# Two products of 64 keys on column halves for one of 128 keys, in the recurrence of the second block's mixers

## The chip, the core and the metric

The kernel is one program on one core of a Trainium2 chip. The metric is the device time of one execution in microseconds; lower is better. Engines: PE is TensorE, DVE is VectorE, ACT is ScalarE, POOL is GpSimd, SP issues the DMAs. One execution was taken by the hardware profiler.

## What is computed

Two transformer blocks on 512 tokens of 1024 features. The first mixes tokens in four ways and has a mixture of experts; the second has two hybrid layers. Each hybrid layer projects its input once and feeds three mixers, differential attention, a gated linear recurrence (HGRN2) in both directions, and attention on a memory, then an output projection and a convolved feed-forward. The change touches the recurrence:

```python
def step(state, inp):
    qt, kt, vt, bt = inp
    o_inter = jnp.einsum('bhtk,bhkv->bhtv', qt * jnp.exp(bt), state)
    diff = bt[:, :, :, None, :] - bt[:, :, None, :, :]
    dec = jnp.where(mask, jnp.exp(jnp.where(mask, diff, 0.0)), 0.0)
    attn = jnp.einsum('bhtk,bhtsk->bhts', qt, dec * kt[:, :, None, :, :])
    o_intra = jnp.einsum('bhts,bhsv->bhtv', attn, vt)
    b_last = bt[:, :, -1:, :]
    state = jnp.exp(b_last[:, :, 0, :])[..., None] * state + jnp.einsum(
        'bhsk,bhsv->bhkv', kt * jnp.exp(b_last - bt), vt)
    return state, o_inter + o_intra
```

There are 4 heads of 128 features each. The second direction runs the same on the flipped sequence.

## The kernel before, in words

`mixers` (L2947) runs once for each of the two layers. The sequence is cut into 4 chunks of 128 tokens. Within a chunk the 128x128 matrix `attn` of each head is built in rounds, since the decay depends on both tokens and on the feature. Round 0 (`round0`, L3178) makes scores for tokens that lie in the same block of 4. Level i (`level`, L3189; i = 1 to 5) makes them for pairs of tokens in the two halves of a block of 2, 4, ... times 4 tokens, so of 8, 16, 32, 64 and 128 tokens, with the decay taken against the block's middle: half_of(i) is 4, 8, 16, 32, 64. In the forward direction (d = 0) the queries are the upper half of a block and the keys the lower one; backward (d = 1) it is the other way round.

For each chunk and head, a round is one product in float32: stationary are the weighed keys of the whole chunk (128 features x 128 keys), moving are the weighed queries (128 in round 0, the 64 of the query side in a level). The result goes to `lev`, called `L` in the code, four PSUM banks of 128x512. A float32 product is two passes, so 16 products are 32 pairs of LDWEIGHTS and MATMUL. A level uses two of the four banks, alternately. DVE then copies with a mask what belongs to the level into `att` (`keep0` L3859, L3865; `keep`, L3878); what lies outside the mask in the banks is computed and not used.

The order of the work is written out by hand for every engine. On PE, between rounds, stands one tile of the input projection, w_in (`tile(n)`, L3138, L3139 and L3144: 24 passes of 128x512 in fp32r), because the recurrence leaves PE waiting otherwise:

```python
round0(0); turn_values(0); tile(10)
for i in range(1, 6):
    level(0, i)
    if i < 4: turn_values(i)
    tile(10 + i)
for h in range(H): turn_keys(0, h)
```

Backward the same stands with `rot(i)` (L3247, one product of the rotary position code) in place of `turn_values`, tiles 21 to 25. `turn_keys` (L3214) and `turn_values` (L3175) are transposes against the identity. DVE's order per level is: `far(d, i+1)` (L3842, L3843: differences of the cumulated decay; they wait for the level that last read that buffer), `weigh(d, i)` (L3857, L3858: keys and queries times the decay; `weigh0` is L3849, L3850), `keep(d, i-1)`, `low_part(n)` (L3779: the low part of a weight tile, which `tile(n)` needs for its last third and which waits for `tile(n-2)`); backward `rope` is added (L3918, L3919, L3921), which waits for the product of `rot` and lets the next `rot` go on. ACT takes each tile's result (L3513), makes the high part of a later one (L3503), and makes the exponentials (L3530 to L3546). After level 5 come `to_end` on DVE (L3884, L3885), an exponential on ACT (L3545, L3546) and `weigh_ends` on DVE (L3889, L3890), on which `turn_keys` waits. `clamp(0)` (L3813, L3814) stands early in the mixers, some 30 us ahead of round 0. SP loads w_in in blocks of 512 KB into a ring of three.

The prediction also reads two places outside the change: `new_state` of the first block's recurrence (L1574, L1575), whose products have 64 stationary and 64 moving columns and whose heads write PSUM partitions 0 to 63 and 64 to 127 in turn, and `token_means` (L3263), whose products have 32 stationary columns and write the four strips of 32 partitions in turn.

Of the kernel before, what the change touches and what calls it, by code (L numbers as in the profile page):

```python
# [14 lines left out]
P = 128  # L15
# [151 lines left out]
@contextmanager  # L167
def stage(nc, *names):

    with ExitStack() as ctx:  # L170
        sems = [ctx.enter_context(nc.semaphore(n)) for n in names]
        with nc.Block() as block:
            yield (block, *sems)
        nc.clear_and_free_semaphores(sems)
        nc.all_engine_barrier()
# [180 lines left out]
def parts_of(K, x, n=S):  # L356

    with ExitStack() as ctx:
# [6 lines left out]
NORM_SEMS = ["x_mean", "x_centred", "x_squared", "x_var", "x_root", "x_inverse", "x_spread", "x_scaled", "x_biased",  # L365
             "x_high", "x_low"]


EARLY_SEMS = ["e_summed", "e_shift", "e_prepared", "e_centred", "e_squared"]
# [2577 lines left out]
def mixers(K, a, layer, x, cs, sn, gain, bias):  # L2947
# [5 lines left out]
    nc = K.nc  # L2953
    lam_init = 0.8 - 0.6 * float(np.exp(-0.3 * layer))
    share = 1.0 - lam_init
    with ExitStack() as ctx:
# [6 lines left out]
        with ExitStack() as c1:  # L2963
# [28 lines left out]
            L = K.ps(c1, "lev", [P, 4, 512])  # L2992
# [5 lines left out]
            z = [quad["z0"], quad["z1"], quad["z2"]]  # L2998
# [50 lines left out]
            def half_of(i):  # L3049
                return 4 << (i - 1)  # L3050

            def query_side(ap, i, d):

                return ap.rearrange("p g (n two m) -> p g n two m", two=2, m=half_of(i))[:, :, :, 0 if d else 1, :]
# [6 lines left out]
            def blocks(t, m):  # L3061
# [7 lines left out]
                     "a_gathered", "a_summed", "a_stored", "m_scored", "m_max", "m_exps", "m_mixed", "m_turned", "m_gathered",  # L3069
                     "m_summed", "m_stored", "d_squared", "d_mean", "d_root", "d_normed",  # L3070
                     "mv_turned", "mv_taken", "yh_ready", "yl_ready", "eps_ready", "w_taken", "positions_in",
                     "turned", "rope_ready"] + EARLY_SEMS + NORM_SEMS
            with stage(nc, *names) as (block, *sems):
                (loaded0, loaded1, loaded2, mem_in, high_ready, low_ready, product, taken, lam_prod, lam_sum,
                 lam_exp, own, lb_diff, lb_ready, gate_in, clamped, logs, k_ready, q_ready, offset, decay,
# [3 lines left out]
                 a_gathered, a_summed, a_stored, m_scored, m_max, m_exps, m_mixed, m_turned, m_gathered,  # L3079
                 m_summed, m_stored, d_squared, d_mean, d_root, d_normed,  # L3080
                 mv_turned, mv_taken, yh_ready, yl_ready, eps_ready, w_taken, positions_in,
                 turned, rope_ready), norm_sems = sems[:-len(NORM_SEMS) - len(EARLY_SEMS)], sems[-len(NORM_SEMS):]
                early = Early(K, x, 6, K.mu[:, :], K.spare[:, :], lambda j: kk[j // 4][:, j % 4, :], sems[-len(NORM_SEMS) - len(EARLY_SEMS):-len(NORM_SEMS)])
                norm = Norm(K, x, gain, bias, X0[:, :], X1[:, :], lambda j: xsq[j // 4][:, j % 4, :], turned_t[:, 0:P],
                            norm_sems, high, low)
# [38 lines left out]
                def _(pe):  # L3124
# [52 lines left out]

                    def round0(d):  # L3178
                        pe.wait_ge(decayed, 14 * d + 2)
                        if d:  # L3180
                            pe.wait_ge(state_ready, 3)
                            pe.wait_ge(put_f, 4)
                        for c in range(NT):
                            s = slice(c * P, (c + 1) * P)
                            for h in range(H):
                                mm = nc.tensor.matmul(L[:, c, h * P:(h + 1) * P], z[1][:, h, s], z[0][:, h, s], start=True, stop=True)
                            mm.then_inc(matched, 1)

                    def level(d, i):  # L3189
                        zz = z[(i + 1) % 3]  # L3190
                        zq = query_side(zz[:, :, :], i, d)
                        n64 = 64 // half_of(i)
                        pe.wait_ge(decayed, 14 * d + 2 + 2 * i)
                        pe.wait_ge(kept, 14 * d + (4 if i < 3 else 2 * i))
                        for j in (0, 1):
                            for cc in (0, 1):
                                c = 2 * j + cc
                                for h in range(H):
                                    g = (cc * H + h) * 64
                                    mm = nc.tensor.matmul(L[:, 2 * (i % 2) + j, g:g + 64], zz[:, h, c * P:(c + 1) * P],  # L3200
                                                          zq[:, h, c * n64:(c + 1) * n64, :], start=True, stop=True)
                            mm.then_inc(matched, 1)

                    def turn_keys(d, h):
# [210 lines left out]
                    for n in range(FIRST_TILES, 10):  # L3415
                        tile(n)
                    round0(0)
                    turn_values(0)
                    tile(10)
                    for i in range(1, 6):  # L3420
                        level(0, i)
                        if i < 4:
                            turn_values(i)
                        tile(10 + i)
# [9 lines left out]
                    rot(0)  # L3434
                    tile(20)
                    round0(1)
                    for i in range(1, 6):
                        level(1, i)
                        rot(i)
                        tile(20 + i)  # L3440
# [330 lines left out]
                def _(dve):  # L3771
                    step = Own(dve, own)

                    def low_part(n):
                        if n >= given:
                            dve.wait_ge(high_ready, n + 1 - given)
                        if n >= 2:
                            dve.wait_ge(product, n - 1)
                        nc.vector.tensor_tensor(wl[:, n % 2, 0:unit_width(n)], raw_of(n), high_of(n), ALU.subtract).then_inc(low_ready, 1)  # L3779
# [20 lines left out]
                    def clamp(d):  # L3800
                        if d:
                            dve.wait_ge(gate_in, 1)
                            dve.wait_ge(k_turned, 4)
                            dve.wait_ge(decay, 10)
                        else:
                            dve.wait_ge(taken, 4)
                        if layer:
                            dve.wait_ge(lb_ready, 1)
                            for h in range(H):
                                step.go(nc.vector.tensor_scalar(kk[d][:, h, :], kk[d][:, h, :], lb[:, 1, d, h:h + 1], lb[:, 0, d, h:h + 1],  # L3810
                                                                ALU.mult, ALU.add))
                            step.all()
                        nc.vector.tensor_scalar(b[:, :, :], kk[d][:, :, :], 2.0 ** -60, None, ALU.max).then_inc(clamped, 1)  # L3813
                        nc.vector.tensor_scalar(z[2][:, :, :], kk[d][:, :, :], 1e-20, 2.0 ** -60, ALU.max, ALU.min).then_inc(clamped, 1)  # L3814
# [188 lines left out]
                        rope_quarter()  # L4003
                    low_part(5)
                    clamp(0)
                    dve.wait_ge(lam_exp, 1)
                    step(nc.vector.tensor_tensor(neglam[:, 0:1], neglam[:, 1:2], neglam[:, 0:1], ALU.subtract))
                    step(nc.vector.tensor_scalar(neglam[:, 0:1], neglam[:, 0:1], lam_init, None, ALU.subtract))
# [389 lines left out]
def second_block(K, a, x, out):  # L4398
    with ExitStack() as ctx:
        cs = K.sb(ctx, "cs", [P, S])  # L4400
        sn = K.sb(ctx, "sn", [P, S])
        K.spare = K.ps(ctx, "x_var", [P, S])
        for layer in range(2):
            first = (lambda t: K.col("ln_in_g_2", t), lambda t: K.col("ln_in_b_2", t))
            later = (lambda t: K.col("ln2_g_2", t), lambda t: K.col("ln2_b_2", t))
            mixers(K, a, layer, x, cs, sn, *(later if layer else first))
            feed_forward(K, a, layer, x, lambda t: K.col("ln1_g_2", 8 * layer + t), lambda t: K.col("ln1_b_2", 8 * layer + t))
        last_norm(K, x, lambda t: K.col("ln2_g_2", 8 + t), lambda t: K.col("ln2_b_2", 8 + t), out)
# [73 lines left out]
```

## Time and profile before

| | us |
|---|---|
| median of 3 runs | 3530.47 (3528.61 to 3533.96) |
| profiled execution, its span | 3526.3 |
| median less that span | 4.2 |
| PE busy | 3363.8 (95%) |
| DVE busy | 2510.4 (71%) |
| ACT busy | 1906.0 (54%) |

The span reaches from the first to the last instruction of the one execution that was profiled; what lies around it in a measured run is not in the profile, so that execution's own time is known only as its span. The mean granted TensorE clock was 0.969 of full speed over the span. A busy PE means that matmuls are in flight; they are pipelined, so the spacing of their starts says more than their durations.

### The profile page before, as it was taken

How to read it: one execution, taken by the hardware profiler on the slowest of the kernel's cores; microseconds unless marked ns; L12 is line 12 of the kernel's file. 1: busy time of each engine (PE TensorE's matmuls, PEld its weight loads, DVE VectorE, ACT ScalarE, POOL GpSimd, SP SyncE). 2: the span in 40 equal slices, each digit the busy share in tenths (PEclk: the TensorE clock that was granted, in tenths of full speed). 3: DMA queues.
4: the chain of work that ended last, by engine and by line, in shares of the span. 5: the costliest groups of instructions: out<-in, count | busy, mean ns of one | idle time of the engine just before them, and what ended most of it. 6: DMA issues, size and time to landing. Idle time of an engine off the chain costs nothing. (4 is left out here: it accounts for less than half of the span.)

```text
span 3526.3 us, 45471 instructions
## 1 busy us (share of the span) xinstructions
PE 3363.8 (95%) x16942; PEld 2708.0 (77%) x16942; DVE 2510.4 (71%) x2900; ACT 1906.0 (54%) x2152; POOL 241.4 (7%) x202
## 2 busy tenths in 40 slices
PE   8998987999999999999989998999999999899998
PEld 6886665888888888888758886778887887678886
DVE  6654566999999999999757766566536775656543
ACT  4223334778777877778646536344415534534422
POOL 0000000122121212121100000000000000000000
PEclk9998997999999999999979999999999999999999
DMA  4110236999999999999812110223331111023331
GB/s 151 49 31 27 64 117 238 363 367 368 365 370 363 369 364 369 369 368 367 291 39 84 60 61 29 68 84 96 107 97 65 62 55 59 24 86 96 97 108 65
DMA packets 118802, 600.28 MB, mean 170 GB/s; under 512 B 20722, under 2 KB 24194, under 8 KB 68130
## 3 DMA queue, kind: packets, MB, share of 16 engines
q1 hardware_dynamic: 105346, 580.93, 45.4%
q0 software_dynamic: 13312, 17.35, 2.0%
q8 instruction: 100, 1.64, 0.2%
q14 instruction: 44, 0.36, 0.0%
HBM read 586.06 MB, written 28.90 MB: 174 GB/s over the span
## 5 line engine op out<-in xcount | busy, mean ns | idle before, releaser
L2486 DVE TENSOR_TENSOR wl<-raw,wh 128x2048 fp32r<-128x2048 f32 x384 | 872.7, 2286 | 52.0 <-ACT wh L2415 52.0
L2415 ACT ACTIVATE wh<-raw 128x2048 fp32r<-128x2048 f32 x384 | 735.6, 1916 | 189.0 <-PE pu L2360 144.4
L2358 PE MATMUL pu<-wh,Xh 128*128 128x512 f32 x1024 | 409.7, 400 | 0.0
L2360 PE MATMUL pu<-wh,Xl 128*128 128x512 f32 x1024 | 399.9, 391 | 0.0
L2359 PE MATMUL pu<-wl,Xh 128*128 128x512 f32 x1024 | 399.8, 390 | 0.0
L4300 ACT ACTIVATE w_high<-w_raw 128x1024 fp32r<-128x1024 f32 (+1 forms) x114 | 131.3, 1151 | 320.4 <-PE acc L4272 161.1
L4347 DVE TENSOR_TENSOR w_low<-w_raw,w_high 128x1024 fp32r<-128x1024 f32 (+1 forms) x114 | 152.4, 1337 | 185.3 <-PE ps L4230 100.0
L4252 PE MATMUL ps<-x_high,w_high 128*128 128x512 f32 x656 | 255.2, 389 | 0.0
L4253 PE MATMUL ps<-x_low,w_high 128*128 128x512 f32 x656 | 255.2, 389 | 0.0
L2358 PEld LDWEIGHTS pu<-wh,Xh 128*128 128x128 f32 x1024 | 192.7, 188 | 45.4 <-issue 8.1
L2360 PEld LDWEIGHTS pu<-wh,Xl 128*128 128x128 f32 x1024 | 192.6, 188 | 42.0
L2359 PEld LDWEIGHTS pu<-wl,Xh 128*128 128x128 f32 x1024 | 193.0, 188 | 37.2
L3138 PE MATMUL acc<-x_high,w_high 128*128 128x512 f32 x528 | 218.5, 414 | 1.5 <-ACT hq L3513 1.5
L2358 PE MATMUL pd<-wh,hh 128*128 128x512 f32 x512 | 208.8, 408 | 0.2 <-DVE hl L2500 0.2
L3139 PE MATMUL acc<-x_low,w_high 128*128 128x512 f32 x528 | 207.6, 393 | 0.0
L2360 PE MATMUL pd<-wh,hl 128*128 128x512 f32 x512 | 200.3, 391 | 0.0
L2359 PE MATMUL pd<-wl,hh 128*128 128x512 f32 x512 | 199.6, 390 | 0.0
L4230 PE MATMUL ps<-x_high,w_low 128*128 128x512 f32 x704 | 173.2, 389 | 0.0
L3779 DVE TENSOR_TENSOR w_low<-w_raw,w_high 128x1024 fp32r<-128x1024 f32 (+1 forms) x102 | 115.6, 1135 | 57.9 <-PE acc L3144 28.3
L4230 PEld LDWEIGHTS ps<-x_high,w_low 128*128 128x128 f32 x704 | 132.1, 188 | 27.4
L4252 PEld LDWEIGHTS ps<-x_high,w_high 128*128 128x128 f32 x656 | 123.1, 188 | 25.6
L4253 PEld LDWEIGHTS ps<-x_low,w_high 128*128 128x128 f32 x656 | 123.1, 188 | 25.5
(784 smaller groups left out, 6837.8 us busy)
## 6 DMA issues: line engine op xcount, KB each, us to landing
raw<-in_exp_w SPq DMA_DIRECT2D x384, 1024.0 KB, 7.6
w_raw<-in_w_in SPq DMA_DIRECT2D x100, 512.0 KB, 3.4
w_raw<-in_w_up SPq DMA_DIRECT2D x82, 512.0 KB, 3.8
w_raw<-in_w_down SPq DMA_DIRECT2D x32, 704.0 KB, 4.0
w_raw<-in_w_out SPq DMA_DIRECT2D x32, 384.0 KB, 3.1
kv_raw<-in_w_mem_kv SPq DMA_DIRECT2D x16, 512.0 KB, 3.7
x<-in_x SPq DMA_DIRECT2D x4, 1024.0 KB, 8.2
w_raw<-in_w_out SPq DMA_DIRECT2D x8, 512.0 KB, 4.9
```

The lines of the kernel that those rows point to most:

```text
L2358: nc.tensor.matmul(o, lh[:, k, :], wh[:, m % PARTS, c], start=(m >= 8 and kh == 0 and kk == 0), stop=False)
L2359: nc.tensor.matmul(o, lh[:, k, :], wl[:, m % PARTS, c], start=False, stop=False)
L2360: mm = nc.tensor.matmul(o, ll[:, k, :], wh[:, m % PARTS, c], start=False, stop=end)
L2415: nc.scalar.activation(wh[:, m % PARTS, :], raw[:, m % RAW, :], ACT.Copy).then_inc(w_high, 1)
L2486: nc.vector.tensor_tensor(wl[:, m % PARTS, :], raw[:, m % RAW, :], wh[:, m % PARTS, :], ALU.subtract).then_inc(w_low, 1)
L3138: nc.tensor.matmul(o, wh[:, n % 3, c], high[:, k, :], start=(k == 0), stop=False)
L3139: nc.tensor.matmul(o, wh[:, n % 3, c], low[:, k, :], start=False, stop=False)
L4230: mm = nc.tensor.matmul(o, wl[:, u % 2, c], high[:, k, :], start=False, stop=(k == DT - 1))
L4252: nc.tensor.matmul(o, wh(u)[:, c], high[:, k, :], start=(k == 0), stop=False)
L4253: nc.tensor.matmul(o, wh(u)[:, c], low[:, k, :], start=False, stop=False)
L4300: nc.scalar.activation(wh(u), raw_of(u), ACT.Copy).then_inc(high_ready, 1)
L4347: nc.vector.tensor_tensor(wl[:, u % 2, 0:width(u)], raw_of(u), wh(u), ALU.subtract).then_inc(low_ready, 1)
```

## The change

Round 0 and levels 1 to 4 make, for each chunk and head, two products of 64 keys in place of one of 128: one with the keys 0 to 63 of the chunk, written to PSUM partitions 0 to 63, and one with the keys 64 to 127, written to partitions 64 to 127, each against only those queries that lie in the same half of the chunk (64 of 128 in round 0, 32 of 64 in a level). Level 5 makes one product of 64 keys: forward the lower half, backward the upper half, against the 64 queries of the other half. What a level wrote outside of that before is no longer written, and so DVE clears the first three banks of `lev` once in each layer, after `clamp(0)`; round 0 waits for it.

```diff
 def round0(d):
     pe.wait_ge(decayed, 14 * d + 2)
+    pe.wait_ge(lev_cleared, 1)
     if d:
         pe.wait_ge(state_ready, 3)
         pe.wait_ge(put_f, 4)
     for c in range(NT):
-        s = slice(c * P, (c + 1) * P)
         for h in range(H):
-            mm = nc.tensor.matmul(L[:, c, h * P:(h + 1) * P], z[1][:, h, s], z[0][:, h, s], start=True, stop=True)
+            for r in (0, 64):
+                s, g = slice(c * P + r, c * P + r + 64), h * P + r
+                mm = nc.tensor.matmul(L[r:r + 64, c, g:g + 64], z[1][:, h, s], z[0][:, h, s], start=True, stop=True)
         mm.then_inc(matched, 1)
...
                 for h in range(H):
                     g = (cc * H + h) * 64
-                    mm = nc.tensor.matmul(L[:, 2 * (i % 2) + j, g:g + 64], zz[:, h, c * P:(c + 1) * P],
-                                          zq[:, h, c * n64:(c + 1) * n64, :], start=True, stop=True)
+                    if i == 5:
+                        r = 64 * d
+                        mm = nc.tensor.matmul(L[r:r + 64, 2 * (i % 2) + j, g:g + 64], zz[:, h, c * P + r:c * P + r + 64],
+                                              zq[:, h, c:c + 1, :], start=True, stop=True)
+                        continue
+                    for side in (0, 1):
+                        r, b0 = 64 * side, c * n64 + side * n64 // 2
+                        mm = nc.tensor.matmul(L[r:r + 64, 2 * (i % 2) + j, g + 32 * side:g + 32 * side + 32],
+                                              zz[:, h, c * P + r:c * P + r + 64], zq[:, h, b0:b0 + n64 // 2, :],
+                                              start=True, stop=True)
             mm.then_inc(matched, 1)
...
     clamp(0)
+    nc.vector.memset(L[:, 0:3, :], 0.0).then_inc(lev_cleared, 1)
     dve.wait_ge(lam_exp, 1)
```

## Rows read from the trace of the kernel before

**Rows 1.** The page, its first part: busy time and share of the span.

```profile
PE 3363.8 (95%) x16942; PEld 2708.0 (77%) x16942; DVE 2510.4 (71%) x2900; ACT 1906.0 (54%) x2152; POOL 241.4 (7%) x202
```

**Rows 2.** Windows, forward then backward: PE, PEld, DVE, ACT, POOL, clock, DMA, GB/s.

```profile
1937.00:1947.00 10.00, 10.00 (x64) 8.95 (x63) 6.23 (x7) 3.95 (x4) 0.00 (x0) 1.00 0.18 52
...
2020.00:2030.00 10.00, 10.00 (x60) 8.48 (x59) 9.93 (x12) 3.85 (x4) 0.00 (x0) 1.00 0.15 54
```

**Rows 3.** Timeline, forward, layer 0: start, length, engine, line; round 0, level 1.

```profile
1909.28 3.73 PE L3186 MATMUL lev<-z,z 128*128 128x128 f32 x32
...
1912.85 0.60 PE L3175 MATMUL x_mu<-const,hout 128*128 128x128 f32 x4
...
1918.78 3.68 PE L3200 MATMUL lev<-z 128*128 128x64 f32 x32
```

**Rows 4.** Timeline of the first block's recurrence: products of 64 columns.

```profile
279.29 0.29 PE L1575 MATMUL G<-vt,ktt 128*64 128x64 f32 x4
...
279.41 0.33 PE L1574 MATMUL G<-x,btt 128*64 128x64 f32 x4
...
279.53 0.33 PE L1575 MATMUL G<-vt,ktt 128*64 128x64 f32 x4
```

**Rows 5.** Timeline, layer 1: from transposes to narrow products and back.

```profile
2927.70 0.60 PE L3258 MATMUL x_mu<-const,dv 128*128 128x128 f32 x4
...
2928.23 0.81 PEld L3263 LDWEIGHTS lev<-z,const 128*32 128x32 f32 x32 [0.17 <-issue]
...
2929.24 0.50 PE L3138 MATMUL acc<-x_high,w_high 128*128 128x512 f32 x1
...
2929.58 0.39 PE L3139 MATMUL acc<-x_low,w_high 128*128 128x512 f32 x1
```

**Rows 6.** Timeline, backward direction, layer 0: levels 1 to 5, DVE's weighing.

```profile
2010.88 3.76 PE L3200 MATMUL lev<-z 128*128 128x64 f32 x32 [2.02 <-DVE att L3865]
...
2020.76 3.65 PEld L3200 LDWEIGHTS lev<-z 128*128 128x128 f32 x32 [0.16 <-DVE z L3858]
...
2028.41 1.22 DVE L3858 TENSOR_TENSOR z<-hfb,z 128x1024 f32<-128x1024 f32 x1
...
2030.54 3.77 PEld L3200 LDWEIGHTS lev<-z 128*128 128x128 f32 x32
...
2037.34 1.22 DVE L3858 TENSOR_TENSOR z<-hfb,z 128x1024 f32<-128x1024 f32 x1
...
2040.46 3.77 PEld L3200 LDWEIGHTS lev<-z 128*128 128x128 f32 x32
...
2050.38 3.77 PEld L3200 LDWEIGHTS lev<-z 128*128 128x128 f32 x32
...
2050.88 1.23 DVE L3779 TENSOR_TENSOR w_low<-w_raw,w_high 128x1024 fp32r<-128x1024 f32 x1 [5.64 <-PE acc L3144]
...
2056.35 1.10 PE L3247 MATMUL x_var<-dk,const 128*128 128x512 f32 x2 [2.06 <-DVE rope_t L3918]
```

**Rows 7.** Layer 1, backward: a window with its granted clock; levels 1, 2 (timeline).

```profile
2843.30:2850.20 6.90, 6.90 (x24) 5.51 (x24) 6.83 (x9) 4.45 (x4) 0.00 (x0) 0.51 0.23 76
...
2841.51 5.40 PE L3200 MATMUL lev<-z 128*128 128x64 f32 x32 [2.04 <-DVE att L3865]
...
2854.54 3.77 PEld L3200 LDWEIGHTS lev<-z 128*128 128x128 f32 x32
```

**Rows 8.** Timeline, forward, layer 0: weigh_ends and the first turn_keys.

```profile
1959.86 2.29 DVE L3889 TENSOR_TENSOR z<-hff,z 128x2048 f32<-128x2048 f32 x1 [4.89 <-ACT ends L3546]
...
1965.24 1.03 PE L3214 MATMUL lev<-const,z 128*128 128x128 f32 x8
```

**Rows 9.** Timeline, DVE around clamp(0) in both layers, and a PSUM copy.

```profile
1879.71 0.16 DVE L4007 TENSOR_TENSOR neglam<-neglam 128x1 f32<-128x1 f32 x1 [3.18 <-ACT neglam L3642]
...
1911.90 2.59 DVE L3865 COPY_PREDICATED att<-const,lev 128x512 f32<-128x512 int32 x4
...
2715.40 2.29 DVE L3818 TENSOR_TENSOR sums<-sums,z 128x2048 f32<-128x2048 f32 x1 [2.28 <-ACT z L3522]
```

More of the change, by code:

```diff
@@ L3071, in mixers @@
                      "mv_turned", "mv_taken", "yh_ready", "yl_ready", "eps_ready", "w_taken", "positions_in",
-                     "turned", "rope_ready"] + EARLY_SEMS + NORM_SEMS
+                     "turned", "rope_ready", "lev_cleared"] + EARLY_SEMS + NORM_SEMS
             with stage(nc, *names) as (block, *sems):
@@ L3081, in mixers @@
                  mv_turned, mv_taken, yh_ready, yl_ready, eps_ready, w_taken, positions_in,
-                 turned, rope_ready), norm_sems = sems[:-len(NORM_SEMS) - len(EARLY_SEMS)], sems[-len(NORM_SEMS):]
+                 turned, rope_ready, lev_cleared), norm_sems = sems[:-len(NORM_SEMS) - len(EARLY_SEMS)], sems[-len(NORM_SEMS):]
                 early = Early(K, x, 6, K.mu[:, :], K.spare[:, :], lambda j: kk[j // 4][:, j % 4, :], sems[-len(NORM_SEMS) - len(EARLY_SEMS):-len(NORM_SEMS)])
```

## The prediction, made before the changed kernel was run

> **What bounds the kernel now.** The page gives PE (TensorE) as busy 95% of the span of 3526.3 us [rows 1]. That share is an average over many stages, so I read the stage that the change touches, the mixers' recurrence, once in each of the two layers. The stage by stage windows tell two different stories [rows 2]: in the forward direction PE is busy all of the 10 us and DVE 6.23 us of them; in the backward one, where DVE also does the rotary work, DVE is busy 9.93 of 10 us. So the forward stages should pay in full, the backward ones only until DVE holds PE back.
>
> **What a stage costs now.** A round or level is 32 pairs of weight load and matmul (16 products in float32, two passes each). Round 0 has its first matmul at 1909.28 and the first matmul of the next stage is at 1912.85: 3.57 us for 32 pairs, 112 ns a pair. The levels stream half as many columns per matmul and take as long: 3.68 us from the first matmul's start to the last one's end, against 3.73 in round 0 [rows 3]. The streamed columns therefore don't set the pace, the 128-column weight load does.
>
> **What a stage will cost.** Round 0 and levels 1 to 4 get 64 pairs of 64 columns, alternately on the lower and upper column half; level 5 gets 32 pairs, all on one half. The nearest rows are a product of the first block, with 64 stationary and 64 moving columns, whose heads go to column halves in turn [rows 4]. There groups of four matmuls start at 279.29, 279.41 and 279.53: 0.12 us for four pairs, 30 ns each. One half alone would then pace at about 60 ns, the other filling in between. I take 30 ns: 64 pairs are 1.9 us; level 5's 32 pairs on one half at 60 ns are 1.9 us as well. Levels stream 32 columns instead of 64, for which no row exists; since the load sets the pace I give that nothing. The bounds per stage are 1.6 us (32 narrow pairs over four strips have their loads done in 0.81 us [rows 5], 25 ns each) and 3.8 us (64 pairs at 60 ns, no overlap between halves).
>
> **What the switch costs.** Before, the first load of a level hid behind the tile's last matmul. Narrow column tiles break the stream. Where transposes over the full array give way to 32-column products, the last wide matmul starts at 2927.70+3x0.11 = 2928.03 and the first narrow one at 2928.23; the spacing before was 0.11, so 0.09 us is lost [rows 5]. On the way back the wide matmul starts at 2929.24 with its load (0.50 us long instead of 0.39) and its successor comes 0.34 us later instead of 0.23: a second 0.09 and an unhidden load of 0.11. With the 64-column load, half of that, unhidden on entry: 0.09+0.06+0.09+0.11 = 0.35 us per stage. Zero and 0.6 us bound it, since the semaphore wait in the same place may be part of the 0.20. A stage falls from 3.57 to 1.92+0.35 = 2.27 us, a gain of 1.3 us. The Trainium skill speaks against the change just here: by "TensorEngine Tiling (Array Packing)", Key Properties, changing the tiling mode drains TensorE. The trace agrees, with the 0.09 us above on either side; were there no drain, the sum would be some 3 us better.
>
> **Forward, both layers.** Six stages (round 0, five levels) of 1.3 us are 7.9 us a layer. What must keep ahead: DVE's 6.23 us of work in 10 leave more room than the 1.3 us by which a stage shrinks, and in DVE's order each weighing stands about a stage ahead of the level that reads it (in the first two stages DVE is full, and lives on that lead). The tightest is the chain at the end: tile(14)'s result on ACT, then the exponential, then weigh_ends, which waits 4.89 us for ACT today; its first half is done at 1959.86+2.29 = 1962.15, and turn_keys, which needs it, starts its matmuls at 1965.24 [rows 8]. That chain moves with tile(14) and turn_keys by one stage more, so of the 3.1 us some 1.8 are left. The DMA queues bring one block of 512 KB per stage and are idle most of the time. Two layers: 15.8 us.
>
> **Backward, layer 0.** Levels 1 to 3 hang on DVE. Level 1 waits 2.02 us for keep0 today and still starts at 2010.88 (all times here less the forward gain); level 2, whose loads start at 2020.76, still waits for the weighing, 0.16 us today [rows 6]. From then on a PE period is (2040.46-2030.54)-1.3 = 8.6 us, and DVE's is 2037.34-2028.41 = 8.93 us. Level 3 starts when DVE's weighing ends, 2028.41+1.22 = 2029.63, not at 2030.54: 0.9 gained; level 4 at 2038.6 instead of 2040.46: 1.9; level 5, which has no far step before it on DVE, at 2047.2 instead of 2050.38: 3.2 us. What follows is clocked by tile(24)'s end: DVE waits 5.64 us for it, then keep(1,4), to_end and rope(4), for which PE's rot(5) waits 2.06 us [rows 6]. Level 5's own gain only lengthens that wait. So 3.2 us.
>
> **Backward, layer 1.** Here the granted clock fell to 0.51 from 2843.3 to 2850.2 (1.2 GHz; PE had just stood waiting for keep0) and level 2 starts at 2854.54 [rows 7]: 833.8 us after layer 0's 2020.76, where level 1, at 2841.51 and 2010.88, is 830.6 us apart; so the fall cost 3.2 us [rows 6, 7]. DVE then has slack, PE is the bound, and levels 1 to 4 give 1.3 us each: 5.3 us.
>
> **The clearing and the waits.** The new memset writes 1536 columns of PSUM from DVE. No row has it; four PSUM copies of 512 columns took 2.59 us [rows 9], so 1.9 us by that, 0.5 us at the least. In layer 0 it lands in a 3.18 us idle of DVE; in layer 1 DVE has 2.28 us of idle a little later and only one weight split between [rows 9], which tile(6) needs at about the time when it will be ready. I take nothing; 0 to 1 us. PE's new wait in front of round 0 is met some 30 us before (the memset follows clamp(0), at the 3.18 us idle at 1879.71), so what queues behind it on PE loses nothing. The 640 more instructions per layer are given nothing.
>
> **Sum.** 15.8+3.2+5.3 = 24.3 us. Against that, PE's idle before level 1 and before rot(5) grows from 2.1 to about 3.5 us, and in layer 1 either idle of today was followed by the low clock; in layer 0 neither was. I deduct 1.5 us for one such fall more. Net 23 us. The profiled execution's span is 3526.3 us and the runs' median 3530.5, 4.2 us of it outside the span, which stays: 3530.5-23 = 3507.5 us.
>
> **Rivals.**
> (B) The halves don't overlap in this order (two passes low, two high, and so on; in the block of [rows 4] four and four). Then a stage of 64 costs 3.8+0.35 us, 0.6 more than today, and level 5 saves 1.3. A layer loses 2x(5x0.6-1.3) = 3.4 us at most, part of it in PE's idle: 3533 us, within the noise. Against it stand the 30 ns of [rows 4] and the 32 pairs in 0.81 us of [rows 5]. 7%. By the Trainium skill, "TensorE: Matmul & The Clock Gate", Wait — 56ns, not 53.3ns?, a sequencer in its ucode mode spends about 62 ns on every MATMUL, whatever its size; by that this would be 3540 us, an estimate. The 30 ns of [rows 4] contradict it.
> (C) Slower: every change of half drains as a change of mode does. Place: 31 changes in each of ten stages a layer. At 0.09 us each a stage costs 2.27+2.8 = 5.1 us, 1.5 more than today; forward 5x1.5-1.3 = 6.2 us, backward some 5 us after PE's idle is used up, both layers about 22 us: 3553 us. It decides from 1.3/31 = 0.042 us per change. For it: a switch that costs 0.09 exists. Against it: the products of [rows 5] change strips at every product, at 25 ns a pair. 4%.
> (D) The backward stages give nothing, by falls of the clock in the longer idles of both layers or by DVE: forward alone, 3514.7 us. For it: the full DVE of [rows 2] and the fall of [rows 7]. 12%.
> (E) Cheaper switches and pairs (no switch cost, 1.7 us a stage): 1.9 us a stage, 22.8 forward and some 11 backward: 3497 us. 10%.
> My forecast has the remaining 67%.
>
> **How the numbers follow.** The likeliest case gives 3507.5. The range 3497 to 3522 takes in D and E, a switch of 0.6 us a stage (0.25 us more in some 20 stages that bind, 5 us), the memset's 1 us and two falls of the clock; B and C lie outside. A measurement can tell about 0.2%, 7 us, from no change. Faster by more than that: A, D, E, 89% less what a sum of small misses takes, 0.88. Within: B, 0.08. Slower: C and B's worse half, 0.04.
>
> **What would show it.** In the new profile the 64-column loads of round 0 and levels should show about 0.14 us, a stage of 64 pairs about 2 us, level 5 the same with half the pairs; a gap of 0.2 us on either side of each; level to level 8.1 us forward where it was 9.4, and about 8.9 backward in layer 0 with new short waits for DVE; weigh_ends still ahead of turn_keys; the memset under 2 us within DVE's idle. A stage of 4 us would be B, of 5 us C. A forward gain per layer under 6 us would make the switch cost wrong; more low clock around the idle before level 1 and rot(5) would be D.

## The result, and the profile after

| | before | changed |
|---|---|---|
| median | 3529.54 us (4 runs) | 3503.28 us (4 runs, 3501.45 to 3505.52) |
| span of the profiled execution | 3526.3 us | 3500.6 us |
| ratio of the runs | | 0.9922 (95% interval 0.9908 to 0.9936) |

The kernel became 26.3 us faster by the medians and 25.7 us by the profiled spans; 3507.5 us was forecast, in a range of 3497 to 3522. In the page, the head answers to [rows 1]. What stands behind the levels in the code has line numbers 10 higher than before (11 behind the clearing); a level is now L3209 (levels 1 to 4) and L3204 (level 5), round 0 is L3188, turn_keys L3224.

```profile
span 3500.6 us, 46757 instructions
PE 3331.6 (95%) x17582; PEld 2668.4 (76%) x17582; DVE 2512.5 (72%) x2902; ACT 1905.5 (54%) x2152; POOL 240.7 (7%) x202
```

PE carries 640 more pairs of weight load and matmul and is busy 32 us less, while its share of 95% hasn't moved: that number says nothing of a stage.

The timeline of the changed kernel, forward, layer 0, answers to [rows 3]; before a name stand start, length, engine and line:

```profile
1905.31 1.97 PE L3144 MATMUL acc<-x_high,w_low 128*128 128x512 f32 x8
...
1907.21 2.08 PE L3188 MATMUL lev<-z,z 128*64 128x64 f32 x64
...
1909.22 0.66 PE L3175 MATMUL x_mu<-const,hout 128*128 128x128 f32 x4
...
1915.30 2.06 PE L3209 MATMUL lev<-z 128*64 128x32 f32 x64
...
1954.72 1.03 PE L3224 MATMUL lev<-const,z 128*128 128x128 f32 x8
```

Round 0 has twice the pairs. From its first matmul's start to its last one's it takes 1.86 us (the 2.08 us less the last matmul's own 0.22), where it took 3.46; that is 29.5 ns a pair. From its first matmul to the next stage's is 2.01 us, against 3.57. The eight wide matmuls ahead of it start 0.227 us apart, the last at 1905.31+7x0.227 = 1906.90, so the entry takes 0.31 us where the stream has 0.23. Levels stream half as many columns and take 2.06 us against 2.08: here too the load sets the pace, not the streamed columns. The last line is the first turn_keys, 47.51 us after round 0, where it was 55.96 us.

The windows answer to [rows 2]:

```profile
1937.00:1947.00 10.00, 10.00 (x100) 8.15 (x98) 6.79 (x7) 3.35 (x3) 0.00 (x0) 1.00 0.21 60
...
2010.00:2020.00 10.00, 9.87 (x123) 7.67 (x121) 9.93 (x13) 4.41 (x5) 0.00 (x0) 1.00 0.15 54
```

In the forward window PE is still never idle and DVE has room. The backward timeline, layer 0, answers to [rows 6]:

```profile
2000.35 2.95 PE L3209 MATMUL lev<-z 128*64 128x32 f32 x64 [3.58 <-DVE att L3875]
...
2017.88 1.22 DVE L3868 TENSOR_TENSOR z<-hfb,z 128x1024 f32<-128x1024 f32 x1
...
2019.15 2.06 PE L3209 MATMUL lev<-z 128*64 128x32 f32 x64
...
2028.10 2.06 PE L3209 MATMUL lev<-z 128*64 128x32 f32 x64 [0.36 <-DVE z L3868]
...
2036.64 2.08 PE L3204 MATMUL lev<-z 128*64 128x64 f32 x32
...
2036.81 1.23 DVE L3789 TENSOR_TENSOR w_low<-w_raw,w_high 128x1024 fp32r<-128x1024 f32 x1 [2.05 <-PE acc L3144]
...
2042.28 2.05 PE L3257 MATMUL x_var<-dk,const 128*128 128x512 f32 x2 [3.57 <-DVE rope_t L3928]
...
2051.16 1.04 PE L3224 MATMUL lev<-const,z 128*128 128x128 f32 x8
```

Levels 3 and 4 start as DVE's weighing ends (2017.88+1.22 = 2019.10), 8.95 us apart, DVE's period. DVE's wait for tile(24) fell from 5.64 to 2.05 us, and PE's wait for rope(4) grew from 2.06 to 3.57 us, just as level 5 shrank.

Where the time went, from the starts of the first matmuls in both traces, in us after the start of round 0 of the same direction and layer:

| | before | changed | gain |
|---|---|---|---|
| forward, to turn_keys, layer 0 | 55.96 | 47.51 | 8.45 |
| backward, to level 5, layer 0 | 45.48 | 41.95 | 3.53 |
| backward, to turn_keys, layer 0 | 58.92 | 56.47 | 2.45 |
| forward, to turn_keys, layer 1 | 55.96 | 47.51 | 8.45 |
| backward, to level 5, layer 1 | 48.79 | 41.95 | 6.84 |
| backward, to turn_keys, layer 1 | 63.40 | 57.67 | 5.73 |

The four stretches to turn_keys give 25.1 us. The remaining 0.6 us lies outside: round 0 of layer 0 already starts 2.1 us earlier than before, and the stretches behind turn_keys give 1.4 us of that back. The early start is no work of the change: in the eleven traces of this case the first round 0 starts anywhere from 1904.1 to 1913.0 us.

The clearing is one memset, in the timeline of DVE in layer 0, and DVE's wait for ACT after it in layer 1 (both answer to [rows 9]):

```profile
1874.68 1.34 DVE L4016 MEMSET lev<- 128x1536 f32 x1 [0.32 <-issue]
...
1877.55 0.16 DVE L4018 TENSOR_TENSOR neglam<-neglam 128x1 f32<-128x1 f32 x1 [1.52 <-ACT neglam L3652]
...
2702.71 2.29 DVE L3828 TENSOR_TENSOR sums<-sums,z 128x2048 f32<-128x2048 f32 x1 [0.64 <-ACT z L3532]
```

It took 1.34 us, with 0.32 us ahead of it. DVE's idle shrank by both together, from 3.18 to 1.52 us in layer 0 and from 2.28 to 0.64 us in layer 1: hidden in both.

### The profile page after: what moved, and what is told of

It is laid out like the page before. It is cut to its first block and busy times, and to the rows that moved or that the text cites. A ratio compares the mean times of both kernels' runs of the same rounds, so it can differ in the third digit from the quotient of the medians.

```text
span 3500.6 us, 46757 instructions
## 1 busy us (share of the span) xinstructions
PE 3331.6 (95%) x17582; PEld 2668.4 (76%) x17582; DVE 2512.5 (72%) x2902; ACT 1905.5 (54%) x2152; POOL 240.7 (7%) x202
```

## The experiments

The code of each is the changed kernel with the edit shown, unless it says otherwise. The medians of the kernel before in the three sets of runs were 3530.06, 3533.39 and 3532.55 us, so across sets the ratios, each to the kernel before, compare better than the times. Times after round 0 are read from one trace of each kernel.

**All of one half, then all of the other.** The same products in another order, in the levels 1 to 4 too. DVE is told of a bank only when its upper half is done.

```diff
-for c in range(NT):
-    for h in range(H):
-        for r in (0, 64):
+for r in (0, 64):
+    for c in range(NT):
+        for h in range(H):
             s, g = slice(c * P + r, c * P + r + 64), h * P + r
             mm = nc.tensor.matmul(L[r:r + 64, c, g:g + 64], ...)
...
```

> The changed kernel with the products of a round or level in another order: first all on the lower column half, then all on the upper one; the same products, the same loads. Theory (what pays is that the two halves run side by side): 32 pairs in a row on one half pace at about 58 ns, so a stage of 64 pairs takes 2 x 1.86 = 3.7 us in place of 1.9, a forward level-to-level period about 9.9 us in place of 8.06, and the whole about 3531 us. Rival (a 64-column product costs about 29 ns by itself, in any order): 1.9 us a stage and 3503 us, unchanged.

Measured: 3529.11 us, ratio 0.9996 (0.9984 to 1.0009); the whole gain is gone. The timeline, round 0 forward:

```profile
1904.09 3.77 PE L3188 MATMUL lev<-z,z 128*64 128x64 f32 x64
```

The same 64 pairs take 3.77-0.22 = 3.55 us in place of 1.86; forward turn_keys stands 55.80 us after round 0 in place of 47.51. Halving the load alone gives nothing, because there are twice as many loads. What pays is that the halves run side by side, and in this order they hardly do. Only at the seam do they overlap: in the single starts, where each half makes a series of its own some 58 ns apart, the first upper matmul is at 1905.777, ahead of the last three lower ones (1905.829, 1905.888 and 1905.946). That is also why the stage took 3.55 and not 3.7 us, and the forward period 9.72 rather than 9.9 us. Orders in between, with groups of 4 or 8 products to a half, were not run.

**Level 5 alone.** Round 0 and levels 1 to 4 with 128 keys.

```diff
+if i < 5:
+    mm = nc.tensor.matmul(L[:, 2 * (i % 2) + j, g:g + 64], zz[:, h, c * P:(c + 1) * P],
+                          zq[:, h, c * n64:(c + 1) * n64, :], start=True, stop=True)
+    continue
 if i == 5:
...
```

> Only level 5 is changed (one product of 64 keys on one half); round 0 and levels 1 to 4 as before the change. Theory (half the columns to load, half the time, and a switch of 0.35 us): level 5 takes 1.9+0.35 us, 1.4 us less than before in both forward directions; backward the level is followed by a wait for DVE and gives nothing. Together 2.8 us less than before: 3526.7 us. Rival (one half alone gains nothing, as the other stands idle): level 5 takes 3.6 us or more and the whole 3530 us.

Measured: 3528.7 us, ratio 0.9992 (0.9981 to 1.0004), which alone can't be told from nothing. The trace can: forward turn_keys stands 54.58 us after round 0 in both layers, 1.38 us less than before. The level in its timeline:

```profile
1959.05 2.08 PE L3207 MATMUL lev<-z 128*64 128x64 f32 x32
```

32 pairs in 1.86 us, 60 ns each: one half's own pace, as forecast. The rival, that one half alone gains nothing, is out.

**One wide product inside each narrow stage.** Round 0 and levels 1 to 4, chunk 1, head 3.

```diff
+if c == 1 and h == 3:
+    s = slice(c * P, (c + 1) * P)
+    mm = nc.tensor.matmul(L[:, c, h * P:(h + 1) * P], z[1][:, h, s], z[0][:, h, s], start=True, stop=True)
+    continue
 for r in (0, 64):
...
```

> The changed kernel, but one of the 16 products of round 0 and of levels 1 to 4 (chunk 1, head 3) is again one of 128 keys, so that each of these stages goes from the halves to the full array and back once more. Theory (a switch of the tiling drains and leaves one load unhidden, 0.35 us for in and out): 0.35+0.22-0.12 = 0.45 us more per stage, a forward period of 8.5 us in place of 8.06, 4 to 8 us more in all (3507 to 3511 us). Rival (the gaps beside the stages are semaphore waits, not drains): 0.1 us more per stage, 3504 us.

Measured: 3512.01 us, ratio 0.9940 (0.9921 to 0.9959). Round 0's timeline:

```profile
1906.10 1.04 PE L3192 MATMUL lev<-z,z 128*64 128x64 f32 x28
...
1907.07 0.30 PEld L3188 LDWEIGHTS lev<-z,z 128*128 128x128 f32 x2
1907.07 0.49 PE L3188 MATMUL lev<-z,z 128*128 128x128 f32 x2
1907.48 1.01 PEld L3192 LDWEIGHTS lev<-z,z 128*64 128x64 f32 x32
1907.48 1.15 PE L3192 MATMUL lev<-z,z 128*64 128x64 f32 x32
```

Then level 2:

```profile
1923.05 1.01 PE L3217 MATMUL lev<-z 128*64 128x32 f32 x28
1923.99 0.44 PE L3207 MATMUL lev<-z 128*128 128x64 f32 x2
1924.35 1.13 PE L3217 MATMUL lev<-z 128*64 128x32 f32 x32
```

In round 0 the last narrow matmul ahead of the island starts at 1906.10+1.04-0.22 = 1906.92, the island 0.15 us after it, and the next narrow one 0.41 us after the island begins, of which two wide pairs are 0.22. There is no semaphore wait in between, so the gaps belong to the switch, and the rival is out. The price depends on the stage. A level period is 8.42 us in place of 8.06: 0.36 us, less the 0.22 and plus the 0.12 of the four narrow pairs left out, 0.26 us for in and out. From round 0 to level 1 it is 8.53 us in place of 8.09: 0.44 us, and by the same sum 0.34 us, about the 0.35 assumed. The two differ in the streamed columns, 64 (128 in the wide product) against 32 (64): the pace of the pairs doesn't show them, the switch does. Forward turn_keys comes 1.9 us later in each layer. The interval of the ratio overlaps that of the changed kernel (0.9908 to 0.9936), so it is the trace that shows the price, not the time.

**Forward only.** The backward direction with 128 keys.

```diff
+if d == 1:
+    mm = nc.tensor.matmul(L[:, 2 * (i % 2) + j, g:g + 64], zz[:, h, c * P:(c + 1) * P],
+                          zq[:, h, c * n64:(c + 1) * n64, :], start=True, stop=True)
+    continue
...
```

> The forward direction as changed, the backward direction with products of 128 keys as before. Theory (forward PE is the bound and gains 1.4 us in each of six stages, backward DVE holds it back and gives some 2.5 us in layer 0 and 5.7 us in layer 1): 16.9 us less than before, 3512.6 us, 9 us more than the changed kernel. Rival (both directions give the same, 13 us each): 3516.5 us.

Measured: 3518.93 us, ratio 0.9967 (0.9954 to 0.9980), 6 us more than the theory gave, and 2 us more than the rival. Forward turn_keys stands at 47.51 us, exactly as in the changed kernel. It is the backward part, whose code is that of before, that came out slower than in the profile of before: 63.45 and 64.99 us to turn_keys where before had 58.92 and 63.40, 6.1 us in all. A window of it, layer 0, and level 1:

```profile
2000.00:2008.00 8.00, 8.00 (x35) 6.74 (x34) 7.93 (x10) 4.50 (x4) 0.00 (x0) 0.57 0.20 68
```

```profile
1999.26 5.84 PE L3207 MATMUL lev<-z 128*128 128x64 f32 x32 [2.03 <-DVE att L3883]
```

After the wait of 2.03 us the clock was at 1.2 GHz most of the window (0.57 granted) and level 1 took 5.84 us. Here the clock fell in both layers; in the trace of before it fell in one of two. So the backward direction with wide products varies by up to 4.5 us in a layer with the clock, and one profile of it isn't its price.

It isn't only the one trace: the median granted clock of the ten runs is 0.9665, against 0.969 in the 29 of the kernel before. By the medians the forward direction alone gives 11 us (7 to 16 by the interval), not the 16.9 us that its own stretches gained, and the backward direction on top of it gives some 16 us (0.9967-0.9922), not 8.2. Both splits add up to about the same whole. Whether a shorter forward direction makes the clock fall more often in a backward one with wide products, or whether it was chance, no run here tells.

**tile(25) before rot(5), backward.**

```diff
-for i in range(1, 6):
+for i in range(1, 5):
     level(1, i)
     rot(i)
     tile(20 + i)
+level(1, 5)
+tile(25)
+rot(5)
 rot(6)
```

> The changed kernel with one thing moved: backward, tile(25) runs before rot(5) in place of after it, so that PE has work while DVE makes to_end and rope(4). Theory (in the changed kernel the gain of backward level 5 is lost in PE's wait of 3.57 us before rot(5), which is also where the clock falls): the wait and the fall go, turn_keys comes some 2 to 4 us earlier after round 0 (56.5 and 57.7 us in the changed kernel) until it waits for weigh_ends and rot(6) for rope(5); 3 to 7 us less than the changed kernel, 3496 to 3500 us. Rival (DVE's chain from tile(24)'s end to weigh_ends sets turn_keys anyway): nothing, 3503 us.

Measured: 3508.43 us, ratio 0.9932 (0.9907 to 0.9958): no gain that can be told. turn_keys came at 56.08 and 56.23 us instead of 56.47 and 57.67. The wait only moved to rot(6), in the timeline of layer 0, and the low clock moved with it (0.72 granted from 2049 to 2055 us in layer 0, 0.50 from 2869 to 2875 in layer 1):

```profile
2049.30 1.94 PE L3257 MATMUL x_var<-dk,const 128*128 128x512 f32 x2 [3.84 <-DVE rope_t L3931]
```

rot(6) needs rope(5), which DVE makes behind weigh_ends. The theory's main part fell; the rival was nearly right.

**Strips of 32 keys.** Levels 1 to 3 are like round 0 below with 16 queries to a strip; level 4 makes two products, at `r = 64 * side + 32 * d`, of the 32 keys of each half that are used.

```diff
-for r in (0, 64):
-    s, g = slice(c * P + r, c * P + r + 64), h * P + r
-    mm = nc.tensor.matmul(L[r:r + 64, c, g:g + 64], z[1][:, h, s], z[0][:, h, s], start=True, stop=True)
+for r in (0, 32, 64, 96):
+    s, g = slice(c * P + r, c * P + r + 32), h * P + r
+    mm = nc.tensor.matmul(L[r:r + 32, c, g:g + 32], z[1][:, h, s], z[0][:, h, s], start=True, stop=True)
...
```

> The changed kernel, carried on: round 0 and levels 1 to 3 make four products of 32 keys on the four strips of 32 columns, level 4 two products of those 32 keys that are used in each half. Theory (four strips side by side, each paced by a 32-column load of 27 ns, so 7 ns a pair): 128 pairs in 0.9 us, a forward period of 7.1 us by PE, held at some 7.5 us by DVE's work in levels 1 to 3; 2.5 to 3.5 us less per layer forward, nothing backward; 3497 us. Rival (starting an instruction costs about 7 ns, two per pair): 14 ns a pair, 128 pairs in 1.8 us as now, 3503 us.

Measured: 3493.75 us, ratio 0.9892 (0.9864 to 0.9919). Timeline, round 0, then levels 1 and 4 forward:

```profile
1907.02 1.35 PE L3188 MATMUL lev<-z,z 128*32 128x32 f32 x128
...
1914.36 1.30 PE L3217 MATMUL lev<-z 128*32 128x16 f32 x128
...
1936.26 1.21 PE L3210 MATMUL lev<-z 128*32 128x32 f32 x64
```

128 pairs run in some 1.15 us, 9 ns each; 64 pairs on two strips in 1.01 us, 16 ns each. The 9 ns lie between the theory's 7 and the rival's 14, nearer to the theory. Forward turn_keys stands at 43.62 us, 3.9 us less than with halves, and the period is 7.30 us: DVE did not hold it back at 7.5, as it was expected to. Backward turn_keys came at 56.38 and 56.29 us in place of 56.47 and 57.67. The ratio's interval just overlaps that of the changed kernel.

**Tiles ahead of the levels, backward.**

```diff
 for i in range(1, 6):
+    tile(20 + i)
     level(1, i)
     rot(i)
-    tile(20 + i)
 rot(6)
```

> The changed kernel with the backward order turned round: each tile(20 + i) runs before level(1, i) and not after it. Theory (backward DVE is the bound once a level is short; PE then stands idle for DVE, and DVE in turn waits 2.05 us for tile(24)): PE's wait before level 1 is filled by tile(21), DVE's wait for tile(24) goes, turn_keys then waits for weigh_ends and for rot(6), some 4 us earlier in each layer; 3495 us. Rival (the backward direction is bound by PE as the forward one is): no change, 3503 us, or later, as the levels come later.

Measured: 3499.7 us, ratio 0.9914 (0.9884 to 0.9944). turn_keys stands at 54.11 us in both layers, 2.4 and 3.6 us less than in the changed kernel. The direction of the theory holds in the trace, where 4 us a layer were expected; the two ratios' intervals overlap, so the time alone doesn't show it.

**Both.**

> The two before together: strips of 32 keys, and tiles ahead of levels in the backward direction. If both theories hold their gains lie in different directions and add: 3489 us. If the backward one falls, 3497 us; if the strips give nothing, 3495 us.

Measured: 3490.82 us, where 3489 was expected if both hold, ratio 0.9876 (0.9854 to 0.9899), with turn_keys at 43.59 us forward and 54.17 backward. In the backward timeline PE now waits most for rope(5), before rot(6):

```profile
2042.21 2.05 PE L3271 MATMUL x_var<-dk,const 128*128 128x512 f32 x2 [5.67 <-DVE rope_t L3942]
```

**turn_keys before rot(6), added to the last one.**

```diff
-rot(6)
 for h in range(H):
     turn_keys(1, h)
+rot(6)
 tile(26)
```

> The kernel of the last run (strips of 32 keys, tiles ahead of levels backward) with rot(6) moved behind turn_keys. Theory (what PE waits for there, 5.67 us, is rope(5), which DVE makes only after weigh_ends, while turn_keys needs only the first half of weigh_ends): turn_keys starts some 49.5 us after round 0 in place of 54.2, 4 us less in each layer, 3482 us. Rival (what comes after is paced by DVE, which is as late as before): turn_keys earlier, the chunks not; 3490 us.

Measured: 3487.27 us, ratio 0.9875 (0.9858 to 0.9891). turn_keys comes at 49.3 us, as the theory says, and the first product of the chunks 68.3 and 68.7 us after round 0 in place of 70.9 and 71.9. The ratio is that of the run before it, so the time doesn't show whether the 2.6 and 3.2 us reach the end. The two traces say that they mostly do: from the first round 0 to the end is 1579.5 us there and 1574.5 us here, and what hides it in the spans is that round 0 started 6.7 us later, behind code that is the same in both. The forecast of 3482 us was 5 us too low. Either of the last two beats both kernels of this case by a margin clear of their intervals.

## Why the prediction was right, point by point

The likeliest case came about, in its mechanism forward and in layer 0 backward. In layer 1 the number was near partly by luck.

*What a stage costs.* The 30 ns a pair from [rows 4] were measured as 29.5, and level 5's 60 ns on one half as 60. Giving the 32 streamed columns nothing was right: levels and round 0 take the same. That the halves overlap, rival (B)'s question, is shown by the grouped order, which takes the whole gain away; what (B) feared came true in an order that the change doesn't have.

*The switch.* Mis-sized, the right way round: 0.35 us assumed. The island gives 0.26 us for in and out of a level and 0.34 us in round 0, and the forward period fell by 9.45-8.06 = 1.39 us, not 1.3. For a level the sum comes out as 3.52-1.87-0.26 = 1.39 us, where I had 3.57-1.92-0.35 = 1.3: 64 pairs take 1.87 us, and a wide level took 3.52 us to the next stage, not the 3.57 of round 0. Of what I put too high in the switch, 0.05 us is the return: I took the unhidden load of the 0.11 us that a wide fp32r tile shows in [rows 5], while behind a narrow stage forward come transposes, whose first matmul is only 0.33-0.27 = 0.06 us longer. "TensorEngine Tiling (Array Packing)" of the Trainium skill has it in Key Properties that changing the tiling mode drains TensorE. The 0.26 us agree in that the change has a price; whether it is a drain they don't tell. Rival (C), that each change of half drains, is out: 1.86 us with 31 changes.

*Forward.* 7.9 us a layer was forecast, 8.45 came; nothing on ACT or DVE got in the way, and even 7.30 us periods were kept.

*Backward, layer 0.* Levels 3 and 4 start when DVE's weighing ends and level 5 at 41.95 us, 3.5 us earlier (3.2 forecast). After PE's wait of 3.57 us the clock was then partly low (0.85 and 0.87 granted in the two windows of 6 us from 2038 on), rot(5) took 2.05 us where it took 1.10, and of the 3.5 us only 2.45 reached turn_keys. The sum had deducted 1.5 us for one such fall; this one cost 1.1.

*Backward, layer 1.* 5.3 us forecast, 5.7 measured to turn_keys, but not by the argued mechanism. I had let the loss of 3.2 us stand as an offset, taken DVE to have slack, and counted four stages of 1.3 us on PE. In fact level 5 gains 6.84 us: the clock fell here too (level 1 took 3.58 us), but a short level hides it, since DVE's weighing for level 2 ends only 15.49 us after round 0 in both layers. Level 2 starts 15.73 and 15.69 us after round 0, where before it was 15.74 and 19.03. From there on DVE holds levels 3 and 4 as in layer 0 (waits of 0.19 and 0.35 us). The timeline of levels 1 and 2 with the end of the weighing:

```profile
2820.44 3.58 PE L3209 MATMUL lev<-z 128*64 128x32 f32 x64 [3.59 <-DVE att L3875]
...
2829.04 1.22 DVE L3868 TENSOR_TENSOR z<-hfb,z 128x1024 f32<-128x1024 f32 x1
...
2830.45 0.72 PE L3209 MATMUL lev<-z 128*64 128x32 f32 x18
```

(The view ends within level 2.) Behind level 5 the clock was low again (0.50 granted from 2862 to 2868 us) and took 1.1 us back, a second fall that the sum didn't have. The two errors went opposite ways, so the near hit of this term is partly luck.

*The clearing.* Priced at 1.9 us by a PSUM copy, 1.34 measured (1.66 with what stands ahead of it), hidden as argued.

*The sum.* 24.3 less 1.5 was forecast, 25.1 measured over the four stretches, net of the clock. The differences: forward 1.1 us more, to level 5 backward 0.3 and 1.5 us more in layers 0 and 1, and 0.7 us more lost to the clock. This split goes by one trace of each kernel; by the medians of the forward-only kernel it is another, and that stays open.

## What to carry to other kernels

Where a product's stationary side is wide and its streamed side narrow, ask whether the load sets the pace: here 128 stationary columns took 110 to 112 ns a pair, with 64 as with 128 streamed columns. Splitting it into column parts paid when the parts alternated in the program, so that they ran side by side, and gave nothing when all of one part came first. Enter and leave such stages seldom: a visit cost 0.26 to 0.34 us. Before pricing a shorter stage, ask on the next engine whether it is already waited for: by the traces the forward direction gave the whole 8.45 us a layer, and the backward one 2.45 and 5.73 us. And where waits are followed by a low clock, don't take one trace for the price.

## What the runs showed of the hardware that was not expected

A half-width part paces at 58 to 60 ns a pair alone, two together at 29.5 ns; four strips of 32 columns at 9 ns a pair together, and two strips at 16 ns: the pace per strip rises only from 32 to 36 ns as four instead of two run.

Matmuls of different halves don't start in the order of the program: in the grouped kernel the first one of the upper half starts ahead of the last three of the lower half, which stand before it.

The low clock follows PE's waits in the backward direction, but not always. With the wait of some 2.0 us before level 1 it fell in five of eight passes (level 2 starting 19.0 us or more after round 0 in place of 15.7 or 15.8; the kernels before, grouped, level 5 only and forward only, two layers each). With the 3.6 us of the changed kernel it fell in both, and level 2 came at 15.7 all the same. That doesn't hold for every short level: with the wide island it came at 18.9 and 17.7 us, with strips of 32 at 17.7 and 17.2. What decides between these, no run here tells.
